# Diffusion transformer step, one core: order of gate and modulation weights in the load ring, and seven unread products in the first steps

## The reference, cut to what matters

```python
ada = silu(cvec) @ w_ada + b_ada                    # 1024 -> 6 * 1024, for two conditioning vectors
sh1, sc1, g1, sh2, sc2, g2 = split(ada, 6)
h = rmsnorm(x) * (1 + sc1) + sh1
p = h @ w_in                                        # 1024 -> 3328, the inputs of four token mixers
ya, yb, yc, yd = pool(p), hyena(p), shortconv(p), attention(p)
gates = sigmoid(h @ w_gate + b_gate)                # 1024 -> 4 * 1024
merged = ga * (ya @ w_br_a) + gb * (yb @ w_br_b) + gc * (yc @ w_br_c) + gd * (yd @ w_br_d)
x = x + g1 * (merged @ w_out)
h2 = rmsnorm(x) * (1 + sc2) + sh2
x = x + g2 * moe(h2)                                # 4 groups of 8 experts, the top group, its top 2
y = rmsnorm(x)                                      # also returned: the context tokens' keys and values
```

## Time and profile before

| | |
|---|---|
| three timed runs, median | 1077.49 us |
| three timed runs, lowest and highest | 1074.04, 1078.62 us |
| profiled execution: time, span | 1080.01, 1078.4 us |
| granted PE clock, mean | 0.975 |
| busy: PE, DVE, ACT, POOL | 1001.9, 567.7, 229.5, 211.7 us |
| read from HBM, written | 203.71, 25.64 MB |

### The profile page before, as it was taken

The page is one execution under the profiler, slowest core; times in us unless marked ns, Lnnn a source line. Parts: engine busy times, 40 slices in busy tenths (PEclk is TensorE's granted clock), DMA queues, the critical chain, the costliest instruction groups (busy, mean ns, idle before and its releaser), DMA issues. The chain is left out here.

```text
span 1078.4 us, 13945 instructions
## 1 busy us (share of the span) xinstructions
PE 1001.9 (93%) x5085; PEld 605.5 (56%) x5085; DVE 567.7 (53%) x1312; ACT 229.5 (21%) x453; POOL 211.7 (20%) x276
## 2 busy tenths in 40 slices
PE   4899999999999999999999999999989999984977
PEld 2457776877655555666666566654555555542432
DVE  4467848143677657777768524145564322322227
ACT  4020001100345454444420100021121111100103
POOL 2350000010493001011111331112131333331100
PEclk9799999999999999999999999999999999997979
DMA  9852121150542343232221651482899999999996
GB/s 320 265 155 78 49 69 40 48 155 32 174 134 90 115 156 118 78 119 78 79 79 65 215 197 40 181 228 117 335 407 406 408 408 408 407 404 407 404 371 274
DMA packets 103540, 218.69 MB, mean 203 GB/s; under 512 B 8710, under 2 KB 64452, under 8 KB 103344
## 3 DMA queue, kind: packets, MB, share of 16 engines
q1 hardware_dynamic: 90000, 187.06, 48.0%
q0 software_dynamic: 12656, 28.07, 7.5%
q10 hardware_dynamic: 816, 2.66, 0.6%
HBM read 203.71 MB, written 25.64 MB: 213 GB/s over the span
## 5 line engine op out<-in xcount | busy, mean ns | idle before, releaser
L2102 PE MATMUL pair<-hT_region,ring_region 128*128 128x512 f32 x192 | 102.8, 618 | 0.0
L988 POOL TENSOR_TENSOR dft_region<-dft_region,padded_region 128x640 f32<-128x640 f32 x24 | 37.1, 1545 | 308.7 <-DVE padded_region L1611 308.6
L2109 PE MATMUL pair<-hT_region,ring_region 128*128 128x320 f32 x336 | 94.8, 435 | 0.1
L2109 PEld LDWEIGHTS pair<-hT_region,ring_region 128*128 128x128 f32 x336 | 62.9, 190 | 29.2 <-issue 3.9
L1995 DVE TENSOR_TENSOR mixer_region<-pair,mixer_region 128x128 f32<-128x128 f32 x32 | 9.3, 291 | 126.4 <-ACT mixer_region L1275 121.1
L2154 PE MATMUL pair<-ring_region,dft_region 128*128 128x512 f32 x160 | 73.1, 607 | 2.4 <-issue 2.3
L2101 PEld LDWEIGHTS pair<-hT_region,ring_region 128*128 128x128 f32 x192 | 37.2, 200 | 56.2 <-issue 53.1
L1010 POOL DMA_INDIRECT moe_pairs<-padded_region,bias_region x30 | 30.7, 1022 | 161.1 <-DVE padded_region L2009 136.1
L1689 DVE SCALAR_TENSOR_TENSOR hyena_region<-ring_region,scT,hyena_region 128x256 f32<-128x256 f32 x112 | 56.1, 501 | 0.0
L1689 DVE SCALAR_TENSOR_TENSOR ring_region<-ring_region,scT 128x256 f32<-128x256 f32 x112 | 55.1, 492 | 0.0
L1275 ACT ACTIVATE mixer_region<-pair 128x128 f32<-128x128 f32 x32 | 8.9, 278 | 199.3 <-PE pair L2483 141.7
(11 more groups left out here) (509 smaller groups left out, 1942.7 us busy)
## 6 DMA issues: line engine op xcount, KB each, us to landing
ring_region<-in_w_ada SPq DMA_DIRECT2D x24, 1024.0 KB, 8.3
ring_region<-in_w_gate SPq DMA_DIRECT2D x16, 1024.0 KB, 7.6
ring_region<-in_w_in SPq DMA_DIRECT2D x13, 1024.0 KB, 5.3
ring_region<-in_w_e_gate SPq DMA_DIRECT2D x11, 1024.0 KB, 12.2
ring_region<-in_w_e_up SPq DMA_DIRECT2D x11, 1024.0 KB, 19.2
ring_region<-in_w_e_down SPq DMA_DIRECT2D x20, 512.0 KB, 16.4
qkv_region<-in_w_e_down SPq DMA_DIRECT2D x17, 512.0 KB, 15.6
hT_region<-in_w_e_gate SPq DMA_DIRECT2D x6, 1024.0 KB, 12.6
```

The lines of the kernel that those rows point to most:

```text
L988: pool.tensor_tensor(merged[:, dj, :], merged[:, dj, :], gtmp, ALU.add).then_inc(merged_add, 1)
L2102: return mm(ps_[0:m, W0 + TC:1024], lhsT, rhs[:, TC:T], start=start, stop=stop)
L2109: ins = mm(out, weights[:, kt, :], columns[:, kt, :], start=(kt == 0), stop=(kt == KD // 2 - 1))
```

## The change

Two things are changed together.

In `loads_of`, a gate step names the gate's weights before the modulation's half (or, for a pair of gates, before its two halves). `LOADS`, and with it the slots and the readers that SP waits for, follow from that. The `gate` step looks up its weights by name, since they are no longer the last in the list.

In `IDLE`, three more entries: two unread products before `("ada", 2)`, two before `("ada", 3)`, one before `("adaT", 3)`; and two more after `("adaT", 3)`, issued behind the semaphore that reports the step.

```diff
     if k == "gate":
         n = step[1] * KD + step[2]
         early = [("ada",) + HALVES[n]] if n in HALVES else []
-        return early + [("gate", step[1], step[2] // 2)]
+        return [("gate", step[1], step[2] // 2)] + early
     if k in ("gp", "gm", "gn", "gq"):
         n = step[1]
         early = [("ada",) + HALVES[i] for i in (n, n + 1) if i in HALVES] if k == "gp" else []
-        return early + [("gate", n // KD, n % KD // 2)]
+        return [("gate", n // KD, n % KD // 2)] + early
...
-            IDLE = {("hb", NT - 1): 1, ("route", NT - 1): 1, ("count",): 5, ("blocks",): 1, ("perm",): 1}
+            IDLE = {("ada", 2): 2, ("ada", 3): 2, ("adaT", 3): 1, ("hb", NT - 1): 1, ("route", NT - 1): 1, ("count",): 5, ("blocks",): 1, ("perm",): 1}
...
                 elif k == "gate":
                     b, dj = st[1:]
-                    w = loaded(pe, loads_of(st)[-1]).rearrange("p (k n) -> p k n", k=KD)
+                    w = loaded(pe, ("gate", b, dj // 2)).rearrange("p (k n) -> p k n", k=KD)
...
                 ins.then_inc(psum_full[n % 4], 1)
+                if st == ("adaT", 3):
+                    keep_busy(p_[:, 512:896], 2)
```

## The result

The changed kernel takes **1069.05 us** (median of 5 runs, 1067.57 to 1069.41) against 1077.4 (5 runs, 1074.04 to 1078.62): ratio 0.9932, 95% interval 0.9913 to 0.9952. The forecast was 1065.6, range 1061.5 to 1073.0: the direction and the range hold, and so do both mechanisms (the waits on gate weights go, the first steps stay at full clock); the time came out 3.5 us above the forecast. The profiled execution took 1069.12 us, span 1067.5; against 1080.01 of before that is 10.9 us less, where 11.9 were forecast.

What follows compares the result with a forecast made beforehand. Up to the expert stage TensorE's chain, 93% busy, was taken as the bound, through its idle waits and half-clock time. Savings of 6.9 + 5.0 = 11.9 us from the median 1077.5 gave 1065.6 us, range 1061.5 to 1073.

Steps and rivals of the forecast that it cites:

- Waits on gate weights, 5.6 us: Branch stage, single gates n = 2, 4, 6, 8: all four TensorE waits on gate weights go, saving 5.6 us.
- Given back at n = 4, 0.4 us: Gate of n = 4: TensorE would now wait for VectorE's merge, which frees the output space; 0.4 us lost, bounds 0 to 1.2.
- Cold products behind the longest wait, 1.7 us: Gate of n = 6: its first two row blocks, slow after the wait, run at full clock, saving 1.7 us.
- part one: Load order in the ring, gate weights ahead of modulation halves: 5.6 + 1.7 - 0.4 = 6.9 us saved.
- Halves late, 0: Gates n = 2 to 8: modulation halves, now issued last, would arrive without stopping TensorE; cost taken as 0.
- Part two, 5.0 us: Seven unread products in the first steps keep the clock up: 5.3 - 0.3 = 5.0 us saved, bounds +5.3 and -3.2.
- The seams: First steps: 0.3 us taken as cost around the unread products, which otherwise fit their gaps at full clock.
- Late next: First steps: the fourth modulation product's weights and ScalarE's sine for the second filter product arrive in time; no new wait.
- The step that was off: Final sum: cold-clock savings of 1.7 and 5.3 us counted in full, later clock falls at nothing, total 11.9 subtracted from the median.
- Rival 2: Cold stretches belong to the profiled execution alone, so only the waits go, less 0.4: 1072.3 us; chance 0.09.
- Rival 1: First steps: the unread products don't keep the clock and cost 3.2 us, load-order gain stays: 1073.8 us; chance 0.13.
- Rival 3: n = 2, 4, 6, 8: modulation halves come too late, delaying VectorE's merge and the gate: 1084.1 us, slower; chance 0.03.

Runs made afterwards that it cites:

- before, first / again: The kernel before, unedited: first profiled and timed at 1077.4 us; profiled and timed a second time at 1077.49 us.
- ring order alone: Changed kernel without the seven unread products in the first steps, keeping gate weights issued ahead of the modulation halves: 1073.16 us, ratio 0.9973.
- products alone: Changed kernel with gate weights and modulation halves back in their old load order, keeping the seven unread products: 1073.1 us, ratio 0.9977.
- after, first / again / third: The changed kernel, unedited, profiled and timed three times: 1069.05, 1068.51 and 1068.81 us.
- four / three products: Changed kernel keeping only the four unread products ahead of `ada` 2 and 3: 1069.05 us; or only the three around `adaT` 3: 1071.25 us.
- narrow: Changed kernel with each of the seven unread 384-column products replaced by three of 16 columns: 1073.38 us, ratio 0.9991.
- the norm's: Changed kernel plus one unread product ahead of the norm's 20 one-column products: 1069.4 us, ratio 0.9930.
- the norm's and `hb` 2's: Changed kernel plus one unread product ahead of the norm and two in the wait ahead of `hb` 2, timed twice: 1067.26 and 1067.52 us.
- the doubled ones: Changed kernel with each of the three groups of unread products doubled, fourteen instead of seven: 1073.77 us, ratio 0.9965.

## Why the prediction held, and where it was off

One sum orders all traces. From the start of the first expert load, take the waits on gate weights, the wait on the merge (L1607), and half of the cold time:

| kernel | first expert load | gate waits | merge | cold | rest |
|---|---|---|---|---|---|
| before, first / again | 757.98 / 754.02 | 5.6 / 5.0 | 0 | 20.5 / 13.6 | 742.1 / 742.2 |
| ring order alone | 746.09 | 0 | 0.8 | 6.8 | 741.9 |
| products alone | 748.72 | 5.8 | 0 | 0 | 742.9 |
| after, first / again / third | 746.82 / 744.73 / 745.15 | 0 | 0.5 / 0.4 / 0.4 | 6.8 / 3.4 / 3.4 | 742.9 / 742.6 / 743.1 |
| four / three products | 746.79 / 749.46 | 0 | 0.4 / 0.6 | 6.8 / 13.6 | 743.0 / 742.1 |
| narrow | 747.91 | 0 | 0.5 | 10.2 | 742.3 |

Thirteen microseconds of difference shrink to 1.2. (The variants with products outside the stops keep those as well: 743.9 with the norm's, 744.8 and 744.4 with the norm's and `hb` 2's, 746.8 with the doubled ones.) So the change works through these two things; anything else is within that 1.2.

- **Waits on gate weights, 5.6 us:** right. All four are gone, and they are back at 5.8 with the old order.
- **Given back at n = 4, 0.4 us:** right, 0.48 at 332.94 on DVE's merge.
- **Cold products behind the longest wait, 1.7 us:** right in the pair of traces. From the gate of n = 0 (281.05 before, 276.92 after) to the first expert load the two differ by 7.0 us; part one was forecast at 6.9. But in the products-alone trace the same 1.8 us wait stands with no fall behind it.
- **Halves late, 0:** right. At n = 6 half (7,0) is issued at 355.64, and DVE's waits name no half anywhere from 225 to 690 us.
- **Part two, 5.0 us:** 5.8 in this pair. Taken between the starts in the earlier trace rows and those above: 0.5 from an earlier start of the transposition, 4.30 - 3.41 = 0.9 on it (forecast 0.8), 11.45 - 9.80 = 1.65 from first to second half (1.7), 7.24 - 4.50 = 2.7 behind that (2.8). The seams cost nothing. Doubling shows that the cover was about used up.
- **Late next:** right. No wait for the fourth modulation product's weights (40.15), and the sine ends at 58.81 + 0.74 = 59.55, the filter product starts at 60.01.

**The step that was off** is the cold time: the sum takes out 1.7 + 5.3 = 7.0 us of it in full and puts later falls of the clock at nothing ("every later fall of the clock may shift" stands in the range only). The last line then subtracts the whole from a median: "The profiled one lies 2.5 us above the median of the three timed runs, 1077.5, so the forecast for the median is 1077.5 - 11.9".

The two first profiles differ by 10.9 us. The missing 1.0 is the 1.7 given back behind the norm, less the 0.8 that part two brought above its forecast, and small change later on. The medians differ by only 8.4, because the first profile of before lay 2.6 above its median, and that of the changed kernel 0.1. The second trace of before, near the median of all, shows a more usual execution:

- It has 3.4 us less of lost time (half of 20.5 - 13.6). Half of that is the fall at 747 us, which the sum had not touched; the other half is cold time around the transposition, of which the sum had counted 0.8. The other cold terms are there again.
- From it to the first trace of the changed kernel the span shrinks by 8.1 us. The time lost to the cold goes from 6.8 to 3.4, which is 3.4 us where the sum had 7.0: that is nearly all that was short.
- The 3.4 left are two falls of 1.7, at 97 and 735 us, where this trace of before has none. Each of the three traces of the changed kernel has one of them or both.

The timed runs say the same by parts: the ring order is worth 4.6 us (0.8) where 6.9 were forecast, 5.2 of them without the cold gate, and the products 4.2 (1.4) where it was 5.0. How often each fall occurs is not known: the runs without a profile don't show their cold stretches, and two and three traces are few.

**Rival 2** was half right. The Trainium skill, page "TensorE: Matmul & The Clock Gate", section "What's actually happening", says that the count of cold matmuls varies between runs of one kernel, and the traces agree: 20.5 and 13.6 us of cold time in two executions of the kernel before. But the products do remove it at the stops they fill (nine traces of nine for each half), which the rival denied. **Rival 1** is refuted by the same traces; its fall of the clock is what the narrow products show. **Rival 3**, late halves, has nothing for it: no wait names a half.

**Open:** the ring order alone has a median of 1073.2 but a profiled execution of 1069.7, so by the sum above its usual execution would be colder by some 7 us than the one seen; only one was traced. Measured against the 35 runs of the kernel before, the two parts alone win 1.8 and 1.9 us and together 6.5, as if they helped each other. Against its twelve runs that were timed as a version of their own, they win 4.7 and 4.4 and together 9.0 by means, which simply adds up. The kernel before drifts by as much between groups (1074.6 to 1077.5), so the gain over it is known to about 2 us, and only the differences between the versions of one group are firm. And why the norm's twenty narrow products are followed by a fall in three of the traces and not in the others is not settled.

## What to carry to other kernels

Before taking cold matmuls out of a sum, profile the kernel twice: the gate waits repeated to 0.6 us, the cold time did not (20.5 and 13.6), and only its average can be subtracted from a median. Leave something for the falls that the changed kernel will have elsewhere. In a kernel bound by TensorE, fill each stop in a row of narrow products with wide unread ones up to the length of the stop and no further: inside it they were free, beyond it each cost 0.6 to 0.7 us. And issue first the load whose reader is on the path.

## What the hardware showed that I had not expected

- Keeping TensorE busy with 16-column products (1.49 us in a stop of 1.5) did not keep its clock at 2.4 GHz; 384-column products in the same places (1.54) did. Twenty one-column records (2.29 us, no idle time) can be followed by 1.2 GHz.
- Most of the kernel's spread seems to be its clock: over twelve runs each it is 11.1 us before, 7.7 with the ring order alone, 6.2 with narrow products, 2.6 with the wide products alone, 1.7 with them doubled. The cold stretches of the single runs were not seen, so this is an inference.
- The 2.02 us put down to "issue" ahead of `hb` 2 was a wait: with two products in it, the trace names ScalarE's turn (L1255) for the 0.49 that remain.
